# Two transformer blocks on one core: columns of the modulation between the slots of the output projection, another order of root and fillers, and an earlier load of the router weights

## The reference, cut to what matters

```python
def first_block(x, c, w_ada, b_ada, ...):
    c_act = jax.nn.silu(c)
    for l in range(DEPTH):                                   # DEPTH = 2
        mod = (c_act @ w_ada[l] + b_ada[l])[:, None, :]      # 1024 -> 6 * 1024
        shift_m, scale_m, gate_m, shift_f, scale_f, gate_f = jnp.split(mod, N_MOD, axis=-1)
        h = rms_norm(x, norm_mix[l]) * (1.0 + scale_m) + shift_m
        x = x + gate_m * hybrid_mixer(h, ..., w_out[l])
        h = rms_norm(x, norm_ffn[l]) * (1.0 + scale_f) + shift_f
        x = x + gate_f * hierarchical_moe(h, ...)
    return x
```

## Time and profile before

| | us |
|---|---|
| median of 3 runs | 3231.29 (3230.54 to 3232.4) |
| time of the profiled execution | 3229.41 |
| span of the profiled execution | 3227.2 |
| PE busy | 3136.6 |
| DVE busy | 2079.7 |
| ACT busy | 1357.3 |

### The profile page before, as it was taken

One profiled execution on the slowest core, in us unless ns is written; L12 is line 12 of the kernel. 1 busy time (PEld: TensorE's weight loads), 2 busy tenths in 40 slices (PEclk: granted clock), 3 DMA queues, 4 the chain that ended last, 5 costly groups with the idle time before them and its releaser, 6 DMA issues.

```text
span 3227.2 us, 46162 instructions
## 1 busy us (share of the span) xinstructions
PE 3136.6 (97%) x15806; PEld 2592.4 (80%) x15806; DVE 2079.7 (64%) x4378; ACT 1357.3 (42%) x2039; POOL 162.5 (5%) x297
## 2 busy tenths in 40 slices
PE   6999999999999999999999999999999999999998
PEld 5688876768887687889888888878788988888887
DVE  5557753545774342899666666665279976666666
ACT  2426642334663243123344444444412334445444
POOL 2100000100000000320000000000032000000000
PEclk8979999999999999999999999999999999999999
DMA  8737887634889632432555555544243255555553
GB/s 296 263 134 287 316 331 302 251 131 153 314 307 347 240 105 74 140 102 80 191 187 189 187 189 188 185 149 146 72 139 105 78 191 190 188 185 191 184 189 122
DMA packets 167141, 614.73 MB, mean 190 GB/s; under 512 B 18752, under 2 KB 18784, under 8 KB 166096
## 3 DMA queue, kind: packets, MB, share of 16 engines
q1 hardware_dynamic: 151632, 551.62, 50.2%
q0 software_dynamic: 15360, 61.16, 5.1%
HBM read 611.66 MB, written 1.05 MB: 190 GB/s over the span
## 4 chain that ended last, share of the span: by engine, by line
PE 86%; DVE 8%; ACT 2%; DMA 1%; DVEq 1%; issue 1%; POOL 0%; ACTq 0%; POOLq 0%
PE PS L1593 13%; PE PS L1595 13%; PE PS L1594 13%; PE PS L2203 11%; PE PS L2204 5%; PE PS L1632 5%; PE PS L2185 4%; PE PS L2166 4%; PE PS L2084 3%; PE PS L1644 2%; PE PS L1886 2%; PE PS L2072 2%; DVE arena L1463 1%; DVE arena L1464 1%; PE PS L1935 1%; DVE arena L1470 1%
## 5 line engine op out<-in xcount | busy, mean ns | idle before, releaser
L2203 PE MATMUL PS<-x_lh,w_hi 128*128 128x512 f32 x1472 | 525.3, 397 | 0.0
L990 DVE TENSOR_TENSOR w_lo<-arena,w_hi 128x1024 fp32r<-128x1024 f32 x440 | 520.9, 1219 | 1.8
L593 ACT ACTIVATE w_hi<-arena 128x1024 fp32r<-128x1024 f32 x440 | 444.0, 1048 | 117.9 <-DMA arena<-in_v_t 79.2
L2204 PE MATMUL PS<-x_lh,w_lo 128*128 128x256 f32 x1472 | 412.8, 280 | 0.0
L1593 PE MATMUL PS<-w_hi,pw_hi 128*128 128x512 f32 x1024 | 406.3, 397 | 6.7 <-DVE w_lo L990 6.2
L1595 PE MATMUL PS<-w_hi,pw_lo 128*128 128x512 f32 x1024 | 402.4, 393 | 0.0
L1594 PE MATMUL PS<-w_lo,pw_hi 128*128 128x512 f32 x1024 | 400.2, 391 | 0.0
L2203 PEld LDWEIGHTS PS<-x_lh,w_hi 128*128 128x128 f32 x1472 | 276.5, 188 | 66.2
L2204 PEld LDWEIGHTS PS<-x_lh,w_lo 128*128 128x128 f32 x1472 | 277.6, 189 | 7.1
L2166 PE MATMUL PS<-x,arena 128*128 128x256 f32 x1024 | 264.3, 380 | 3.9 <-ACT arena L879 3.9
L930 ACT ACTIVATE arena<-PS 128x256 f32<-128x256 f32 x184 | 71.1, 387 | 441.2 <-PE PS L2204 441.2
(11 more groups left out here) (413 smaller groups left out, 5156.1 us busy)
## 6 DMA issues: line engine op xcount, KB each, us to landing
arena<-in_u_t SPq DMA_DIRECT2D x256, 512.0 KB, 4.5
arena<-in_v_t SPq DMA_DIRECT2D x256, 512.0 KB, 3.5
raw<-in_w_gu SPq DMA_DIRECT2D x192, 512.0 KB, 5.3
arena<-in_w SPq DMA_DIRECT2D x152, 512.0 KB, 3.5
arena<-in_w_ada POOLq DMA_DIRECT2D x96, 512.0 KB, 7.3
raw<-in_w_down SPq DMA_DIRECT2D x96, 512.0 KB, 5.4
arena<-in_w_gu SPq DMA_DIRECT2D x64, 512.0 KB, 7.1
arena<-in_w_down SPq DMA_DIRECT2D x32, 512.0 KB, 5.1
```

Source lines behind the costliest of these rows:

```text
L593: A(w_hi[:, m % RING], ring[:, m % RING], ACT.Copy).then_inc(S["hi_done"], 1)
L990: V.tensor_tensor(w_lo[:, m % RING], ring[:, m % RING], w_hi[:, m % RING].bitcast(F32), ALU.subtract)\
L2203: mm(PS[:, 4 + j % 4, :], hi, x_lh[:, :, k], start=k == 0, stop=False)
L2204: last = mm(PS[:, 4 + j % 4, T:2 * T], lo, x_hi[:, k], start=False, stop=k == KT - 1)
```

## The change

What it does, part by part:

- In `mix(0)` DVE runs the modulation steps 8 to 15 directly behind steps 0 to 7, and multiplies x with the root afterwards. PE gets 24 filler matmuls between the columns of m = 0 and those of m = 1.
- The block of 32 columns ahead of the output projection is gone. The eight columns of m = 2 stand between the matmuls of slot 0 of the projection, one behind each of the first seven and one behind the slot; the 24 columns of m = 3 to 5 stand the same way in slots 1 to 3 (seven in each, three behind slot 3). In layer 0 the first eight columns of layer 1 stand in slot 7 in the same way. `ada_mod` is split to match (m = 2 ahead of the first pair's sum, m = 3 to 5 ahead of the third).
- DVE's 16 modulation steps of layer 1 stand four ahead of each pair's sum.
- The router weights are loaded by POOL at the start of the mixer, behind three other small loads, to a place of their own in SBUF.
- Banks: the columns write banks 4 and 5 in place of 7 and 5, and the fillers of the expert stage bank 5 in place of 4.

```diff
@@ -97,6 +97,9 @@
 SPLIT_EXPERTS = len(MU_OF) - len(SHARED)
+
+
+ADA_CALLS = [(0, 1), (0, 2), (0, 3), (0, NMOD), (1, 1), (1, 2), (1, 3), (1, NMOD)]
 
@@ -265,7 +268,8 @@
         E = area([("rs", (T,)), ("sq", (8, T))])
-        E |= area([("sg", (2, FT, P)), ("wr", (KT, NG + NE))], 32000)
+        E |= area([("sg", (2, FT, P))], 32000)
+        E |= area([("wr", (KT, NG + NE))], RING_AT + 13 * SLOT)
         E |= area([
@@ -537,6 +541,7 @@
                     pool.dma_start(M["sbmask"], a["tab"][:, 0:384]).then_inc(S["tab_load"], 16)
+                    pool.dma_start(E["wr"], a["w_rt"][l]).then_inc(S["rt_load"], 16)
                     if l == 0:
@@ -551,10 +556,6 @@
                         peer_ids(l)
-                if kind == "moe":
-
-                    pool.wait_ge(S["x_ready"], s)
-                    pool.dma_start(E["wr"], a["w_rt"][l]).then_inc(S["rt_load"], 16)
 
@@ -968,7 +969,7 @@
                 mod, ga = mods[:, l], gas[:, l]
-                dve.wait_ge(S["ada_ps"], 3 * l + min(m1, 3))
+                dve.wait_ge(S["ada_ps"], ADA_CALLS.index((l, m1)) + 1)
                 V.tensor_tensor(mod[:, KT * m0:KT * m1], PS[:, bank, KT * m0:KT * m1], c1(l, "b_ada", KT * m0, KT * (m1 - m0)), ALU.add)
@@ -995,8 +996,8 @@
                     ada(0, 0, KT)
+                    ada(0, KT, ADA_FIRST)
                     norm(s, M["rs"])
-                    ada(0, KT, ADA_FIRST)
                     ada_mod(0, 0, 2, 6)
@@ -1092,16 +1093,18 @@
                 V.tensor_tensor(M["mixT"][:, 4:8], o2, M["gr"], ALU.mult).then_inc(S["mixb_ok"], 1)
-                ada_mod(l, 2, NMOD, 7)
+                ada_mod(l, 2, 3, 4)
                 for j in range(4):
+                    if l == 0:
+                        ada(1, 4 * j, 4 * j + 4)
+                    if j == 2:
+                        ada_mod(l, 3, NMOD, 5)
                     dve.wait_ge(S["slot_done"], n0 + W1_IN + 2 * j + 2)
...
                     last.then_inc(S["pair_evac"], 1)
-                    if l == 0:
-                        ada(1, 5 * j, min(5 * j + 5, ADA_FIRST))
                 dve.drain().then_inc(S["x_ready"], 1)
@@ -1169,7 +1172,7 @@
                 if l == 0:
-                    ada_mod(1, 0, 2, 5)
+                    ada_mod(1, 0, 2, 4)
 
@@ -1605,11 +1608,18 @@
 
-            def ada_cols(l, m0, m1, bank):
+            def ada_steps(l, m0, m1, bank):
+
                 pe.wait_ge(S["ada_acc"], 3 * l + min(m1, 3))
...
                     last = mm(PS[:, bank, j:j + 1], ADA["acc"][:, j // KT, P * (j % KT):P * (j % KT) + P], ones[:, 0:1], start=True, stop=True)
-                last.then_inc(S["ada_ps"], 1)
+                    if j == KT * m1 - 1:
+                        last.then_inc(S["ada_ps"], 1)
+                    yield j
+
+            def ada_cols(l, m0, m1, bank):
+                for _ in ada_steps(l, m0, m1, bank):
+                    pass
 
@@ -1618,7 +1628,7 @@
 
-            def pairs(n0, p0, n, rhs, ready=None):
+            def pairs(n0, p0, n, rhs, ready=None, between=None):
 
@@ -1631,7 +1641,12 @@
                                       start=k == 0, stop=k == KT - 1)
+                            if between and k < KT - 1:
+                                next(between.get(2 * j + q, iter(())), None)
                         last.then_inc(S["slot_done"], 1)
+                        if between and between.get(2 * j + q) is not between.get(2 * j + q + 1):
+                            for _ in between.get(2 * j + q, ()):
+                                pass
                     yield j
@@ -1652,6 +1667,7 @@
                     ada_cols(0, 0, 1, 6)
+                    filler(24, 3)
                     ada_cols(0, 1, 2, 6)
@@ -1769,14 +1785,15 @@
                 heads(1)
-                ada_cols(l, 2, NMOD, 7)
                 pe.wait_ge(S["outa_ev"], 2 * (l + 1))
                 pe.wait_ge(S["mixb_ok"], l + 1)
-                for j in pairs(n0 + W1_IN, p0 + 8, 4, M["mixT"]):
+                rest = ada_steps(l, 3, NMOD, 5)
+                between = {0: ada_steps(l, 2, 3, 4), 1: rest, 2: rest, 3: rest}
+                if l == 0:
+                    between[7] = ada_steps(1, 0, 1, 4)
+                for j in pairs(n0 + W1_IN, p0 + 8, 4, M["mixT"], between=between):
                     if j:
                         squares(("moe", l), E["sq"], j - 1)
-                if l == 0:
-                    ada_cols(1, 0, 1, 5)
                 squares(("moe", l), E["sq"], 3)
@@ -1796,7 +1813,7 @@
                 pe.wait_ge(S["row_load"], 16)
-                filler(12, 4)
+                filler(12, 5)
                 for t in range(TT):
@@ -1824,8 +1841,8 @@
                 if l == 0:
-                    ada_cols(1, 1, 2, 5)
-                filler(6, 4)
+                    ada_cols(1, 1, 2, 4)
+                filler(6, 5)
 
```

## The result

The changed kernel takes 3239.65 us (median of 13 runs, 3234.62 to 3246.32), the kernel before, run beside it, 3231.07 (13 runs, 3228.72 to 3236.72): ratio 1.0027, 95% interval 1.0020 to 1.0034. It is 8.6 us slower and lies above the forecast range. The profiled execution took 3237.62 us.

A forecast was written before the change was run, and what follows sets the result against it. PE, busy 3136.6 of 3227.2 us, was taken as the bound, so its waits and half-clock stretches counted. Gains 2.3 + 0.5 + 4.0 + 0.4 = 7.2 us took 3231.29 to 3224.1 us, range 3217 to 3231.

The forecast's parts named there:

- clock term: Pairs behind the idle gap: half clock loses between nothing and about 5 us; 2.0 taken in layer 0.
- B: Pairs of layer 0, columns moved between their matmuls: gain 0.5 us (-2.5 to 6).
- D: Layer 1: pairs lose 0.4 us, router starts 0.8 us earlier; gain 0.4 us (-2 to 3.5).
- hidden loads: Rival: a column costs only 0.115 us between pair matmuls, saving another 8.2 us, 3216 us; chance 0.05.
- A: Start of the kernel: earlier tile 0.9, norm beside columns 0.8, clock 0.6; gain 2.3 us (0.4 to 6.0).
- C: Norm and router of layer 0: no wait for weights 1.8 us, plus half of 4.4; gain 4.0 us (-0.4 to 6.2).
- the mixture is too thin: Rival: clock stays at 1.2 GHz through slots 0 to 3, 19 us per layer; 3262 or 3243 us; chance 0.08.
- The norm beside the columns: Start: norm on DVE beside the columns, 2.77 us in place of 3.59 ahead of ada_mod; gain 0.8 us.
- L1675: Start: 16 instructions, L1659 before, took 6.49 us at half clock; gain 0.6 of a possible 2.4 us.
- DVE's lateness: End of layer 0's pairs: DVE's sums no longer end late, gain 2.6 us.
- best case of 6.2: Norm and router of layer 0 all at full clock: 8.9 us in place of 15.1, gain 6.2 us.

The follow-up runs named there:

- e3: Changed kernel with 14 filler matmuls in the 3.3 us gap ahead of the first pair, in both layers; 3213.78 us.
- e6: Changed kernel with 14 fillers and four of the real columns in the gap, and 8 fillers at the start; 3213.78 us.
- e11: Changed kernel with the 14 fillers in the gap of layer 0 alone; 3229.24 us.
- e16: Changed kernel with 14 fillers in both gaps, plus 8 fillers ahead of the last means of the first sparse mixer's output norm; 3217.90 us.
- e5: Changed kernel, gap left idle, columns sparser: one behind every second pair matmul, over slots 0 to 6; 3221.72 us.
- e9: Kernel before, unchanged, for a second trace; 3228.97 us.
- e10: Changed kernel, unchanged, for a second trace; 3239.53 us.
- e7: Kernel before with only the router weights' load moved to the start of the mixer; 3221.69 us.
- e13: Changed kernel with 4 fillers ahead of the last means of the first sparse mixer's output norm; 3243.15 us.
- e14: Changed kernel with 8 fillers ahead of the last means of the first sparse mixer's output norm; 3242.18 us.
- e15: Kernel before with 10 fillers ahead of the last means of the first sparse mixer's output norm; 3232.16 us.
- e2: Kernel before with only the columns of m = 2 to 5 moved between the matmuls of slots 0 to 3; 3242.18 us.
- e4: Kernel before with only the new order of steps and root at the start and the 24 fillers; 3230.12 us.
- e12: Changed kernel with 16 columns as a block behind the heads, the other 16 one behind every second matmul of slots 0 to 3; 3216.45 us.
- e1: Changed kernel with the 32 columns back in one block between heads and pairs of each layer; 3221.57 us.
- e8: Kernel before with only DVE's 16 steps ahead of the sums and the eight columns in slot 7; 3226.75 us.

## Why the prediction was wrong

**The step that failed is the clock term of B and D**: "The loss then is bounded by nothing and by about 5 us ... I take 2.0". Heads to the end of the second pair of layer 0 took 188.91 - 154.65 = 34.3 us, where I counted 3.3 + 13.8 + 7.4 + 2.0 = 26.5. The first three terms were right: the gap is 3.30, a pair matmul and its column at full clock take 0.65 us, of which 0.43 is the matmul, so the column costs 0.22 as counted. What is left for the clock is 34.3 - 24.5 = 9.8 us, 20.5 us at half speed. (So the rival "hidden loads" did not come either.) My bound was the loss of a stretch that ended in pair matmuls alone. I took the length of the half clock as given, when it hangs on the mixture behind the gap.

By the traces, B and D missed by 8.7 and 4.8 us, 13.5 together; A and C gave 2.8 us more than their terms, and code with no term took 6.4 us more. That makes 17.1 us, between a forecast gain of 7.2 and a loss of 9.8. The medians missed by 15.5. This was the rival "the mixture is too thin", to which I gave 0.08, at half its price: it put the half clock at slots 0 to 3 as a whole, and it ended at slot 2. Its argument against, that a pair instruction streams for 0.216 us of each 0.33, was no argument for a clock that is already down. The cause is shown from both sides: without the gap the same mixture keeps the clock (e3, and e6, e11, e16), with the gap and sparser columns it is back after 3.4 us (e5). That the warning of the Trainium skill ("TensorE: Matmul & The Clock Gate", Why this matters for your kernels) on idle gaps between bursts speaks against this part was said; the trace agrees with it: behind 3.30 us of idleness the granted clock fell to 1.2 GHz at 158.6 us. What that cost hung on what followed the gap, 20.5 us at half clock behind one mixture and 3.4 us behind the sparser one.

By parts, from the table above:

- **A**, 2.3 predicted, 3.5 measured (4.1 to ACT's first scaling in the first trace). The tile came 3.2 us earlier, where I took 0.9: its issue moved by 2.9 us, and it landed as much earlier and a little more. My bound of 0.3 us counted only the idle 17% of 26 to 28 us. The same row shows 219 GB/s, against 412 in the row of 18 to 20 us, and I did not read it. From 24 to 34 us before moved 315 GB/s (314 in e9) and the changed kernel 403 (403 in e10 too), 2.2 us worth of transfers. So most of the gain fits transfer time that before left unused; nothing here shows that latency was the limit. The norm beside the columns gave its 0.8. L1675 gave none of 0.6: it ran at half clock for 6.46 us, as before.
- **B**, gain 0.5 predicted, loss 8.2 measured. DVE's lateness went as predicted, and slot 7's columns kept full clock.
- **C**, 4.0 predicted, 5.6 measured: the wait for the weights is gone (e7 has that part alone), and the fillers and router ran at full clock (2.84 us for 24 instructions), near the best case of 6.2.
- **D**, gain 0.4 predicted, loss 4.4 measured: pairs -5.9 (3.4 in the trace with 10.2 us at half clock, 8.4 in the one with 20.5), router +1.5 where I had 0.8.
- **Nothing predicted** for the rest: +1.3 - 0.7 in the expert stages, and +5.8 us in common code.

The 5.8 us are open as to their cause, but the traces show where they lie. This code took 1946 or 1947 us in four traces of the changed kernel (with e13 and e14), and 1939 to 1942 in three of before (with e15). There are four places in it, 123, 276, 1180 and 1333 us behind its start, in the tables of the small experts, where PE waits about 2 us (for ACT at two of them, for DVE at the other two) and the clock can fall for 3.4 us. In the changed kernel's first trace they are the half clock from 1401.1, 1554.7, 2459.2 and 2612.8 us. Set beside e2, which has none of the four, each costs 1.3 to 2.3 us:

| trace | of the four | stretch, us |
|---|---|---|
| e2 | 0 | 1939.4 |
| before, e4, e15 | 1 each | 1939.2, 1939.3, 1940.6 |
| e5 | 2 | 1942.6 |
| e7, e9 | 3 | 1942.0, 1942.2 |
| e16, e12 | 3 | 1944.7, 1945.9 |
| changed, e10, e13, e14, e1, e3, e6, e8, e11 | 4 each | 1946.1 to 1947.4 |

Both traces of the changed kernel have all four, those of before one and three. That makes between 3 and 4 of the 5.8 us; most of the rest, 1.9 us, lies 940 to 1100 us behind the start. It isn't the columns between slots 0 to 3, since e2 had 1939.4 and e1, without them, 1946.3. It isn't the load of the router weights alone (e7), nor the new start alone (e4). The part that is left is e8's: all twelve traces with DVE's steps ahead of the sums and the columns in slot 7 took 1942.6 us or more, all six without them 1942.2 or less, and e8, which has only that part, 1946.1. That is a pattern found afterwards in single traces, and no run shows how such a part could act 600 us and more later.

With e3's fillers in the gap the change is what it might have been: 3213.78, 16.3 us faster than the kernel before by the runs beside it. It and e6 (the same median, 17.6 us) are the best versions found.

## What to carry to other kernels

Work that covers an idle gap of TensorE has a second value, the clock: before moving it, look for what else keeps TensorE busy there, and if there is nothing, put fillers in its place. Here 3.4 us of fillers in a gap of 3.3 us, in each of two layers, were worth some 25 us. When a clock term enters a sum, don't bound it by how long the half clock lasted in a stretch with other instructions; ask what follows the gap. One-column matmuls one behind every second matmul did far better here than one behind each. Judge a part by stretches of the trace beside its median: four parts measured one by one here add up to 2 us of gain, and together they lost 8.6.

## What the runs showed of the hardware that I had not expected

- The same mixture of matmuls (one 128x256 float32 matmul, one of a single column, 0.65 us together at 2.4 GHz) keeps 2.4 GHz when it begins at it (e3, no half clock; seven stretches of seven) and mostly keeps 1.2 GHz for 20 us when it begins behind 3.3 us of idleness (ten stretches of eleven). The share of busy time doesn't tell the two apart, PE is busy for 4.00 of each 4 us in both; the granted clock and the count of matmul instructions do, 26 against 14.
- A DMA share near 1 doesn't say that the transfers run at full rate: before had a share of 0.83 at 219 GB/s from 26 to 28 us, and of 0.92 at 315 GB/s from 24 to 34 us, where the changed kernel had 1.03 at 403 GB/s. The tile issued 2.9 us earlier landed 3.2 us earlier.
- A block of bare one-column matmuls brings the clock down with PE busy all the time: 32 of them for 10.2 to 13.7 us (fourteen stretches), 16 of them for 6.8 us (two).
- Executions of one kernel differ by 8 to 15 us (before 8.0, changed 11.7, e2 15.0), and a stretch of 1940 us that no edit touches took 1939 to 1947 us, mostly by how often the clock fell for 3.4 us at four waits, each worth 1.3 to 2.3 us.
